# Mixer stages issued between the main products of the input projection and of the first output pair

## The reference, cut to what matters

```python
mod = silu(c) @ w_ada + b_ada                    # six vectors: shift, scale, gate, twice
h = rms_norm(x, g_attn) * (1 + scale1) + shift1
u_conv, q_g, k_g, v_g, q_w, k_w, v_w = split(h @ w_in)         # 1024, 768, 256, 256, 768, 256, 256 columns
q_g, k_g = rms_norm(q_g, q_norm), rms_norm(k_g, k_norm)        # per head of 128
y_conv = silu(layer_norm(depthwise_conv31(a * sigmoid(gate)) + b))   # a, gate: halves of u_conv
y_g = attention(q_g, k_g, v_g)                   # 6 heads, 2 key heads; latent tokens: rotary, cached keys too
y_w = attention(q_w, k_w, v_w, sink)             # the same with a learned sink
x = x + gate1 * (concat(y_conv, y_g, y_w) @ w_out)
h2 = rms_norm(x, g_mlp) * (1 + scale2) + shift2
x = x + gate2 * (relu(h2 @ w_mlp1) ** 2 @ w_mlp2)
```

## Time and profile before

| | us |
|---|---|
| median of 3 runs | 2440.06 (2438.89 to 2440.91) |
| the profiled execution, its own time | 2436.85 |
| its span, first to last instruction | 2435.2 |
| PE busy | 2295.0 (94%) |
| DVE busy | 1518.7 (62%) |
| ACT busy | 1064.2 (44%) |
| mean granted TensorE clock | 0.975 |

### The profile page before, as it was taken

The page is one execution under the profiler, slowest core; times in us unless marked ns, Lnnn a source line. Parts: engine busy times, 40 slices in busy tenths (PEclk is TensorE's granted clock), DMA queues, the critical chain, the costliest instruction groups (busy, mean ns, idle before and its releaser), DMA issues.

```text
span 2435.2 us, 36896 instructions
## 1 busy us (share of the span) xinstructions
PE 2295.0 (94%) x13206; PEld 1826.7 (75%) x13206; DVE 1518.7 (62%) x2606; ACT 1064.2 (44%) x1663; POOL 101.6 (4%) x196
## 2 busy tenths in 40 slices
PE   5699879989999999999998997798999999999998
PEld 1277657767887887887786775586788888888886
DVE  0457775575665665565566678767566666666665
ACT  1343334454443443444444342455444545445443
POOL 2000000000000000000000000000000000000000
PEclk9699989999999999999999999999999999999999
DMA  9888645969579669768855885255956555555652
GB/s 386 331 332 300 243 180 211 320 242 324 182 244 319 231 198 314 254 196 294 295 183 204 301 318 214 97 187 189 313 198 196 176 193 186 182 194 176 193 188 87
DMA packets 390556, 570.29 MB, mean 234 GB/s; under 512 B 9604, under 2 KB 364472, under 8 KB 365624
## 3 DMA queue, kind: packets, MB, share of 16 engines
q1 hardware_dynamic: 360504, 365.51, 46.5%
q0 software_dynamic: 27648, 201.34, 20.5%
q10 hardware_dynamic: 2304, 2.10, 0.2%
HBM read 565.76 MB, written 3.15 MB: 234 GB/s over the span
## 4 chain that ended last, share of the span: by engine, by line
PE 86%; DVE 7%; DMA 4%; ACT 2%; issue 1%; POOL 0%; DVEq 0%; ACTq 0%; POOLq 0%
PE bank L466 52%; PE bank L468 26%; PE bank L403 6%; DMA ada<-in_w_ada 4%; DVE hs L1051 1%; DVE ybuf L1043 1%; DVE qrs L938 1%; DVE yconv L901 1%; DVE lo L808 1%; PE bank L483 0%; ACT prob L759 0%; DVE yT L1076 0%; PE bank L421 0%; PE bank L390 0%; PE bank L511 0%
## 5 line engine op out<-in xcount | busy, mean ns | idle before, releaser
L466 PE MATMUL bank<-hs,hi 128*128 128x512 f32 x2944 | 1067.6, 406 | 18.6 <-DVE hs L1051 9.9
L808 DVE TENSOR_TENSOR lo<-raw,hi 128x1024 fp32r<-128x1024 f32 x685 | 816.6, 1222 | 402.2 <-ACT hi L622 401.4
L622 ACT ACTIVATE hi<-raw 128x1024 fp32r<-128x1024 f32 x685 | 706.3, 1054 | 502.7 <-PE bank L468 497.4
L466 PE MATMUL bank<-act,hi 128*128 128x512 f32 x2560 | 908.0, 400 | 5.4 <-DVE act L989 5.4
L468 PE MATMUL bank<-hs,lo 128*128 128x256 f32 x2944 | 830.5, 282 | 0.0
L466 PEld LDWEIGHTS bank<-hs,hi 128*128 128x128 f32 x2944 | 557.9, 189 | 220.4 <-issue 56.4
L468 PE MATMUL bank<-act,lo 128*128 128x256 f32 x2560 | 719.3, 281 | 0.0
L466 PEld LDWEIGHTS bank<-act,hi 128*128 128x128 f32 x2560 | 482.4, 188 | 131.5 <-issue 6.7
L468 PEld LDWEIGHTS bank<-hs,lo 128*128 128x128 f32 x2944 | 560.9, 191 | 2.5 <-issue 2.5
L468 PEld LDWEIGHTS bank<-act,lo 128*128 128x128 f32 x2560 | 484.8, 189 | 0.0
L667 ACT ACTIVATE tmp<-bank 128x256 f32<-128x256 f32 x344 | 113.5, 382 | 443.9 <-PE bank L468 443.9
(11 more groups left out here) (127 smaller groups left out, 712.9 us busy)
## 6 DMA issues: line engine op xcount, KB each, us to landing
raw<-in_w_mlp SPq DMA_DIRECT2D x256, 1024.0 KB, 5.8
ada<-in_w_ada POOLq DMA_DIRECT2D x168, 1024.0 KB, 7.4
raw<-in_w_in SPq DMA_DIRECT2D x56, 1024.0 KB, 5.4
raw<-in_w_out SPq DMA_DIRECT2D x32, 1024.0 KB, 5.3
pre_a<-in_w_ada POOLq DMA_DIRECT2D x16, 1024.0 KB, 18.4
pre_q<-in_w_ada POOLq DMA_DIRECT2D x8, 1024.0 KB, 18.7
xtok<-in_x_prompt SPq DMA_DIRECT2D x1, 1024.0 KB, 14.2
xtok<-in_x_sample SPq DMA_DIRECT2D x1, 1024.0 KB, 32.5
```

What stands on the lines that cost most here:

```text
L466: pe.matmul(bank[:, :], hi[:, h, k, j * P:(j + 1) * P], acts[:, k_, :], start=(k_ == 0), stop=False)
L622: act.activation(hi[:, o % 4, :, :], raw[:, (o // 2) % 4, 4 * (o % 2):4 * (o % 2) + 4, :], ACT.Copy).then_inc(hi_ready, 1)
L808: dve.tensor_tensor(lo[:, o % 4, :, :], raw[:, (o // 2) % 4, 4 * (o % 2):4 * (o % 2) + 4, :], hi[:, o % 4, :, :].bitcast(f32), ALU.subtrac ...
```

## The change

The seven input pairs and the first output pair become one stretch of 64 slices ("steps", numbered 0 to 63) in `mixers`, written for each engine. After the products of a step, PE does `mix_ops(step)`; ACT and DVE first make the `hi` or `lo` slice three steps ahead and then do theirs. The stages `gate`, `qk_norms` and `attention` are gone.

- The columns are reordered (`IN_COLS`): the convolution's channels with their gates, keys and first queries, remaining queries, values, windowed keys and queries. The tile `zq` shrinks from 20 to 12 tiles, which are reused.
- The ada units of the stretch: two behind slice 2 of each half and one more behind slice 0 of halves 9, 11, 12 and 13. `mod_ps` now shares a bank with `ada_ps`, and the first unit of a vector waits for `mods_done` of the one before.
- Norms of queries and keys: the sums go over tokens on the partitions, as sixteen products with one column of ones; ACT's root and DVE's reciprocal work on at most eight columns. Four products spread the keys' factors; the queries' factors go into the exponential's scale and the maxima.
- ACT normalises the probabilities and copies their transposes, both DVE's before. One score bank instead of two: the scores of head e wait for the exponentials of head e-1.
- The taps, each two operations of 128x256 on two channel tiles: in steps 10 to 17 two a step (tiles 0, 1), in 18 to 31 one for tiles 0, 1 and one for 2, 3, in 32 to 45 one for 2, 3 (two at 33 and 34). So 10 to 31 have four operations a step. Two of the same tile lie two operations apart, four before.
- Heads are started every two steps from step 34; each head's link to the next engine is one or two steps later. Rotations go in eight pieces of two tiles instead of four of four.
- The first output pair takes the row blocks in the order 1, 0, 2, 3 (`OUT_CHUNKS`): heads 0 to 3 first, then the convolution. Its halves alternate block by block; SP loads its pieces in the order 0, 2, 1, 3.
- The dummy root `warm` is gone.
- In every pair, those of up and down too, the four products of a k-tile are issued as long, long, short, short instead of long, short, long, short.
- At the end ACT forms `xT * g_final` during the last pair and PE transposes it there (tiles 0 to 11); the factor of the token is applied after the transposes by DVE (two operations of 128x1024) and ACT (four of 128x512), and SP stores four pieces of 512 KB.

```diff
-IN1, IN2, IN3, OUT, UP, DOWN = 2, 3, 2, 4, 4, 4
+IN, OUT, UP, DOWN = 7, 4, 4, 4
+IN_COLS = ((0, 512), (256, 768), (1792, 1024), (1280, 1536), (2048, 3072), (2304, 2560), (2816, 3328))
+OUT_CHUNKS = (1, 0, 2, 3)
+SINGLE_UNITS = (9, 11, 12, 13)
...
+    def units_behind(step):
+        half = step // 4
+        done = 2 * half + sum(x < half for x in SINGLE_UNITS)
+        if step % 4 == 0 and half in SINGLE_UNITS:
+            return [done]
+        if step % 4 == 2:
+            done += half in SINGLE_UNITS
+            return [done, done + 1]
+        return []
...
@@ tensor: the pair @@
                                 for j in range(2):
-                                    k_ = 4 * h + k
-                                    bank = pb[2 * g + j]
-                                    pe.matmul(bank[:, :], hi[:, h, k, j * P:(j + 1) * P], acts[:, k_, :],
+                                    pe.matmul(pb[2 * g + j][:, :], hi[:, h, k, j * P:(j + 1) * P], acts[:, k_, :],
                                               start=(k_ == 0), stop=False)
-                                    mm = pe.matmul(bank[:, TOK:2 * TOK], lo[:, h, k, j * P:(j + 1) * P],
+                                for j in range(2):
+                                    mm = pe.matmul(pb[2 * g + j][:, TOK:2 * TOK], lo[:, h, k, j * P:(j + 1) * P],
                                                    acts[:, k_, 0:TOK], start=False, stop=(k_ == KT - 1))
...
@@ tensor: mixers @@
+                    for step in range(8 * IN):
+                        p, g, h = step // 8, step // 4 % 2, step % 4
+                        if h == 0:
+                            after(pe, bank_freed, 4 * (n + p) + 2 * g - 2)
+                        pe.wait_ge(lo_ready, 8 * n + step + 1)
+                        for k in range(4):
+                            if step < 4:
+                                pe.wait_ge(hs_ready, 2 * l * NORM_STEPS + 8 * h + 2 * (k + 1))
+                            mm = slice_products(g, h, k, h, hs, h + k == 0, h + k == 6)
+                        mm.then_inc(half_used, 1)
+                        for u in units_behind(step):
+                            unit(l, u)
+                        mix_ops(l, step)
...
+                    if step in (45, 48, 52):
+                        r = 5 + (step - 43) // 4
...
+                        exchange(l, r, WIN_Q[2 * (r - 5)])
...
+                    for e in range(2 * HEADS):
+                        if step == turn_step(e):
+                            turn_probs(l, e)
+                    for e in range(2 * HEADS):
+                        if step == values_step(e):
+                            values(l, e)
+                    for e in range(2 * HEADS):
+                        if step == score_step(e):
+                            scores(l, e)
...
@@ scalar: mix_ops @@
+                    for e in range(2 * HEADS):
+                        if step == turn_step(e) + 1:
+                            drain_probs(l, e)
+                    for e in range(2 * HEADS):
+                        if step == score_step(e) + 3:
+                            normalise(l, e)
+                    for e in range(2 * HEADS):
+                        if step == score_step(e) + 2:
+                            exps(l, e)
...
-                    act.activation(warm[:, :], eps[:, :], ACT.Sqrt)
...
@@ plan of the steps @@
+def score_step(e):
+    return 34 + 2 * e
+def turn_step(e):
+    return score_step(e) + 4 if e < HEADS else (50, 52, 54, 57, 58, 59)[e - HEADS]
+def values_step(e):
+    return (40, 42, 44, 46, 49, 50, 58, 58, 59, 59, 60, 60)[e]
+ROPES = ((26, KG), (28, QG), (30, QG + 2), (34, QG + 4), (42, KW), (46, WIN_Q[0]), (49, WIN_Q[2]), (53, WIN_Q[4]))
```

More of the change, by code:

```diff
@@ L235, in walk @@
         first, final = layer == 0, layer == DEPTH - 1
-        a_in = a + PRE_JOBS if first else a + AHEAD
         stage("norm1", 0)
[L238 to L249, removed]
+        mixers(layer)
+        n += IN
+        for i in range(1, OUT):
             pair("out", n + i, i, -1, a + 16 + i if first else None, False)
@@ L351, in _ @@
[L351 to L356, removed]
-            sp.wait_ge(y_stored, 8 * 16)
+                        after(sp, lo_ready, 8 * n - 8 + (3, 7, 4, 8)[s] if kind == "out" and i == 1
+                              else 8 * n + 2 * s - 6)
@@ new lines, in load_pair @@
+                        load(s, w_of[kind][bass.ds(first_row + (s % 2) * (D // 2), D // 2),
+                                           bass.ds(first_col + (s // 2) * 256, 256)])
+                walk(sp, l, load_pair, lambda name, c: None, load_mixers)
+            for s in range(S):
+                for part in range(2):
+                    cols = slice(part * (D // 2), (part + 1) * (D // 2))
+                    sp.wait_ge(y_scaled[part], (s + 1) * (1 + part))
+                    sp.dma_start(t["y"][s].rearrange("a q d -> (a q) d")[:, cols],
+                                 xtok[:, s, cols]).then_inc(y_stored, 16)
@@ new lines, in turn4, with sums @@
+                def turn4(tiles):
+                    for v, tile in enumerate(tiles):
+                        mm = pe.transpose(pb[7][:, v * P:(v + 1) * P], tile, ident)
+                    mm.then_inc(turn_ready, 1)
+                def sums(col, tiles):
+                    for c, tile in enumerate(tiles):
+                        for s in range(S):
+                            mm = pe.matmul(kq_sums[:, col + 2 * c + s:col + 2 * c + s + 1], tile[:, s * P:(s + 1) * P],
+                                           ones[:, 0:1], start=True, stop=True)
+                    mm.then_inc(kq_summed, 1)
@@ L664, in pair @@
                         act.wait_ge(half_used, 8 * n + 4 * g + 4)
-                        for j in range(2):
-                            after(act, bank_freed, 4 * n + 2 * g + j - 1)
-                            act.activation(tmp[:, j, :], pb[2 * g + j][:, TOK:2 * TOK], ACT.Copy)\
-                               .then_inc(tmp_ready, 1)
+                        copies(n, g)
                         for j in range(2):
@@ L868, in pair @@
                             else:
[L869 to L875 removed]
+                                residual(kind, i, g, j)
                         for j in range(2):
@@ L1084, in head, with turns_before, tap_plan @@
     kv = h // GROUP
-    return win, h, (QW if win else QG) + h, (KW if win else KG) + kv, (KV if win else 0) + kv
+    return win, h, WIN_Q[h] if win else QG + h, (KW if win else KG) + kv, (KV if win else 0) + kv
+def score_step(e):
[4 more added lines that the diff above has]
+    return (40, 42, 44, 46, 49, 50, 58, 58, 59, 59, 60, 60)[e]
+def turns_before(e):
+    return 2 + (turn_step(e) > 43) + (turn_step(e) > 56)
+def tap_plan():
+    plan = [{}, {}]
+    a, b = iter(range(1, TAPS)), iter(range(1, TAPS))
+    for step in range(10, 18):
+        plan[0][step] = [next(a), next(a)]
+    for step in range(18, 32):
+        plan[0][step] = [next(a)]
+    for step in range(18, 46):
+        plan[1][step] = [next(b), next(b)] if step in (33, 34) else [next(b)]
+    count, n, done = {}, 0, {}
+    for step in range(8, 48):
+        if step in (9, 17):
+            for ch in (0, 1) if step == 9 else (2, 3):
+                n += 1
+                count[0, ch] = n
+        for first in range(2):
+            for tap in plan[first].get(step, ()):
+                for ch in (2 * first, 2 * first + 1):
+                    n += 1
+                    count[tap, ch] = n
+        done[step] = n
+    assert n == TAP_OPS and next(a, None) is None and next(b, None) is None
+    return plan, count, done
+HEAD_GROUPS = (0, 1, 2, 3, 4, 5, 6, 8, 10)
+TAP_PLAN, TAP_COUNT, TAPS_DONE = tap_plan()
+ROPES = ((26, KG), (28, QG), (30, QG + 2), (34, QG + 4), (42, KW), (46, WIN_Q[0]), (49, WIN_Q[2]), (53, WIN_Q[4]))
 def mix_tile(e):
```

882 lines of the change are left out of this document (520 added, 362 removed).

## The result

| | before | after |
|---|---|---|
| median, us | 2439.55 (4 runs) | 2342.37 (2341.49 to 2342.78, 4 runs) |
| span of the profiled execution | 2435.2 | 2341.1 |
| PE busy | 2295.0 (94%) | 2253.7 (96%) |
| mean granted TensorE clock | 0.975 | 0.981 |

What follows compares the result with a forecast made beforehand. PE, busy 94% of the span, was taken as the bound. 2436.85 - 81.9 + 1.8 + 10.6 - 3.0 = 2364.4 for the profiled execution; the median, 3.2 us above it, was forecast at 2367.6, range 2338 to 2400.

Steps and rivals of the forecast that it cites:

- rival A: All couples: the new order is faster because a long slot's excess from sharing a bank vanishes; -137, time 2230; chance 0.12.
- Step 1 and 3, the waste: Two mixer stretches: PE's waits and lower clock there go, -81.9 us; waits that are left add +10.6.
- step 3: Waits left in the mixers: 4 us a layer, plus 1.3 for the table load at norm2's root; +10.6 in all.
- Step 2: PE work added by the new order in the mixers: spreading the keys' factors, 0.9 us a layer; +1.8.
- Step 3, DVE: Steps 10 to 31: DVE needs 12.0 us a half against PE's 13.3, later stays level with cover; cost nothing.
- Rival B: Mixers: DVE or the chain sets the pace, 27 to 41 us of waste stays, time 2395 to 2409; chance 0.12.
- Step 4, the end: End of the kernel: gain of 5.6 us, less 2.6 for transposes in the last pair; -3.0 (between -8 and +2).
- Step 5, the order: Long, long, short, short in all 86 pairs: no change, 0, with bounds -137 and +220.
- Rival D: All pairs: weight loads don't finish under adjacent short products; up to +220, about 2588 us; chance 0.04.
- Rival C, the clock: Mixer stretches: small products between main ones make the granted clock fall to 0.93; loss 34 us, time 2402; chance 0.05.

Runs made afterwards that it cites:

- experiment 1: The changed kernel with the old order of the four products (long, short, long, short) in all couples: 2364.05 us, ratio to before 0.9692.
- experiments 5 and 6: The changed kernel with one more DVE maximum of 128x1024, result unused, in each of steps 10 to 31: 2368.4 us; once a half only: 2341.66 us.
- experiments 1 and 2: The first: old product order in the changed kernel, 2364.05 us. The second: long, long, short, short in the kernel before, 2416.25 us, ratio 0.9913.
- experiment 3: The changed kernel with the products ordered long 0, long 1, short 1, short 0, so some follow one into their own bank: 2342.7 us.
- experiment 12: The kernel before with 32 small products ahead of PE's first real product, which shift its later instructions in memory: 2452.99 us, ratio 1.0058.

## Why the prediction was right, point by point

The forecast was 2367.6 in a range of 2338 to 2400; measured 2342.4. The mechanism that carried the sum is shown: the signs that I named for it came true, with PE's granted clock at 1.00 in the mixers (1278 to 1513 us, 125 to 364.7), 253.4 us from the first input product to the end of the first output pair in layer 1 where I had 256, and eight table loads a layer. That the number fell inside the range is in part luck. It lies outside the forecast's own range (2355 to 2380) and inside the stated one only because I had drawn that down for a fifth of rival A, and the chunk did shrink, which I had named as A's sign. Without the new order it is 2364.05 (experiment 1), near the forecast, but there 9 us of waits that I had not foreseen stand against a larger gain in the mixers.

- **Step 1 and 3, the waste.** Forecast -81.9 + 1.8 + 10.6 = -69.5; measured without the order -76.5 (experiment 1). Two items of step 3 were too large. The waits that are left are 0.6 and 0.4 us, not 4 a layer: no wait of PE at a single unit is in the list, and of the table loads only the last two can have reached PE, with the 0.4 us at scores (L687, at 334.89, behind a load at 332.35). The load ahead of norm2's root costs 0.15 a layer, not 1.3:

```profile
447.08 1.28 ACT L992 ACT_TABLE_LOAD   x1
...
447.58 0.60 PE L429 MATMUL bank<-ones,ssq 128*128 128x1 f32 x4 [2.68 <-DVE ssq L1110]
...
448.38 0.26 ACT L992 ACTIVATE tok_std<-bank,eps 128x2 f32<-128x2 f32 x1
```

  I had it begin when the sum is ready. It begins when ACT's queue reaches it, right behind the last square (447.07), and the root behind it waits for the sum: of 1.28 us, 1.1 lie beside DVE's last addition and PE's sums. The root starts 0.80 after the sum's first product (447.58 to 448.38); in the kernel before, with the table loaded, it was 0.65, and the difference is the 0.15:

```profile
488.84 0.61 PE L386 MATMUL bank<-ones,ssq 128*128 128x1 f32 x4 [2.68 <-DVE ssq L888]
...
489.49 0.26 ACT L772 ACTIVATE tok_std<-bank,eps 128x2 f32<-128x2 f32 x1 [1.16 <-PE bank L386]
```

  The 2.7 us that I had from the Trainium skill (ScalarE: Activation LUTs, "What ACT_TABLE_LOAD costs") are there a load of 1283 ns and a drain of about 1380. The trace agrees on the load, and shows ACT idle for only 0.01 us ahead of it and 0.02 behind it. With these two items as measured the sum would have been -78.6, 2.1 more than the gain that was measured (with 0.4 for layer 1, 2.3 more); that rest I leave to the change-overs between main and small products, which I had charged at nothing. It is a remainder, not a measurement.
- **Step 2.** Nothing in the rows speaks against it; it was not measured by itself.
- **Step 3, DVE.** Right, and shown by adding load until it was felt (experiments 5 and 6). Rival B is refuted at the present load, and the margin is now bounded: one operation of 1.2 us a half is free, four are not.
- **Step 4, the end.** Forecast -5.6 for the end and +2.6 in the last pair; the end gave 6.7, and the last pair takes 24.8 where it took 22.5 (24.9 in experiment 1, with the old order).
- **Step 5, the order.** Forecast 0 between -137 and +220; measured -22 (experiments 1 and 2). This is the term of the sum that was mis-sized most. I took the nearest row for a value when the rows held a hint of a loss: the couple at the upper clock is 0.353 where half of the lower clock's 0.64 is 0.32. Rival A had the sign and the wrong mechanism: its excess of 0.025 in the long slot is not the bank's (experiment 3), and only about a sixth of it went (22 of 137 us). Rival D is refuted: with eight short products in a row a slot is 0.12, not 0.19. By the rule that I took from the Trainium skill (TensorE: Matmul & The Clock Gate, "Back-to-back issue gap") a couple should take 0.325; the best order here takes 0.348, so some 0.023 stays unexplained, in a stream of fp32r products with a weight load for each. The section gives that rule for a product in isolation, and for a stream with weight loads 0.131 a product of 512 columns; the 0.233 here are far above that, and nearer to the rule.
- **Not in the sum: the place of the program.** +9.7 us by two waits at back jumps (200.8 and 200.6 against 195.8). No row of the kernel before could show them, since it had none; experiment 12 shows that it could have had them.
- **Rival C, the clock.** Refuted: 0.99 in both stretches with the norm's slow start included, against 0.96 before; 1.00 in the mixers behind that start, where the stages that are gone had 0.90 and 0.93. The Trainium skill's case of a clock that swings with short idling (the same page, "A second HAM failure mode: psum-queue depth-cycling") does not arise here: PE is busy 239.0 of 239.7 us there, small products included.

The parts add up: -76.5 for the mixers, -6.7 for the end, +2.4 for the transposes in the last pair and +9.1 for the jumps, all between the kernel before and experiment 1, and -22.6 for the order (spans of experiment 1 and of the changed kernel) make -94.3; the spans differ by 94.1.

## What to carry to other kernels

A stage that is all latency between engines can be laid into a stretch bound by one engine almost without loss, if each link of its chain gets one slice of that engine's work and every other engine stays below the bound engine's pace in each part of the stretch, not on average; check the load part by part, as half by half here. The order of products of unequal length within an accumulation is worth an experiment of its own: two and two took 1.3% less per couple than one and one, and more grouping gave nothing. Before a difference of half a per cent is put down to a change, compare undisturbed stretches of both traces and the packets of the instruction queue, and shift the program once.

## What the runs showed of the hardware that I had not expected

- Long and short products: alternating long (512 columns) and short ones (256) costs 0.0047 us a couple (198.2 against 195.8 us for 512 couples), with either bank; runs of eight are no better than runs of two (2345.3 against 2342.4 us).
- The back jump of this long loop is free or costs PE some 3.3 us of standing and 5 us in all, by the place of the program: 65 or 66 instruction packets of 16 KB in the one case, 83 or 84 in the other, nine more for each of two jumps. In the kernel before the same shift added 7.7 and 6.9 us to two chunks. What decides between the two stays open; the good places are shifts of 32 and 48 products, the bad ones 0, 16 and 64, in both senses for one program only.
- A table load on ACT (1.28 us) runs ahead of the wait of the instruction that needs it, so where that instruction has to wait anyway it is nearly free (0.15 us ahead of norm2's root).
